# Thirty-two dense tokens in place of sixteen take their U activations from fetched rows, and modulation dots move out of layer 0's V stage

## The chip, the cores and the metric

The kernel runs on one core of one Trainium2 chip. The metric is the device time of one execution in microseconds, as the median of several runs; lower is better. Engines are named as in the profile: PE multiplies matrices (PEld is its weight load), DVE is the vector engine, ACT the scalar engine, POOL is GpSimd, SP (SyncE) issues DMAs.

## The reference, cut to what matters

A trunk of two layers works on 512 tokens of width 1024 in float32. Layer 0 mixes with an mLSTM and a gated convolution, layer 1 with stick-breaking attention; both are conditioned by modulation vectors (`ada_params`, one dot of length 1024 for each of 6144 values a layer). After each mixer comes the channel mixer, which is where nearly all of the time goes:

```python
def peer_ffn(h, w_query, sub_keys1, sub_keys2, expert_u, expert_v):
    # 8 heads, 16 picks each: 128 of 16384 experts a token
    ...
    expert = e1 * PEER_NKEYS + e2
    gate = jax.nn.softmax(top_v.astype(jnp.float32), axis=-1).astype(h.dtype)
    ...
    def block(args):
        xt, et, gt = args
        act = jax.nn.gelu(jnp.einsum("td,thkd->thk", xt, expert_u[et]), approximate=False) * gt
        return jnp.einsum("thk,thkd->td", act, expert_v[et])
```

The expert tables U and V have 16384 rows of 1024 floats, 64 MB each.

## The kernel before

**Two ways to do the channel mixer.** For the 384 "dense" tokens (DENSE_T) the kernel multiplies the whole table: in the U stage 128 tiles of U (each 128 experts, 512 KB) meet the tokens' h, the gelu of all activations is stored to DRAM (gel_dram), and in the V stage 128 tiles of V meet the activations times the gates, most of which are zero. Floats are split into a high and a low part, so each product is three matmuls (high by high, high by low, low by high). For the last 128 tokens, "fetched", the 128 picked rows of U and V are gathered by indirect DMA, one row for each token at a time (128 partitions, one token each), and DVE computes a dot (U) or adds a scaled row (V).

**The dense tokens with fetched U rows.** The last EXTRA = 16 of the dense tokens take no part in the U matmuls: their width is DENSE_U = 368. Their activations come from fetched rows as well, 16 gathers of 128 partitions (8 groups of picks by 16 tokens). SP spreads their picks and shares over the groups (`spread_extra`), ACT copies their h out of PSUM (L1185) and SP copies it to the other groups (`copy_extra`); DVE's dots read it as h_extra, from SBUF (`dot`, L2355), where the fetched tokens' h lies in PSUM (h_rows, shown as gbank). The activations get gelu, share and a transpose (L2413), 8 small DMAs (`gather_extra`) bring them into place, and they then act as the gates of these tokens, for which gel holds ones. In V these tokens are like all other dense ones.

**The U stage by engine.** A tile is 8 steps of three matmuls (L1364 to L1366). ACT rounds the raw tile to w_hi (L840), w_lo is the rest, by POOL (L737) nearly to the end of U, afterwards and in V by DVE (L2315), always two tiles or more ahead. ACT takes the gelu out of PSUM (L1114). Beside the first 26 tiles (U_EARLY) DVE picks the experts (L2249 to L2307). From tile 26 on the gate matrices are made beside the tiles: DVE's one-hots (L2326) and planes (L2331) and ACT's low planes (L1153) of four tokens, PE's gate pairs of two tokens (L1745, at places that `pair_step` writes into the tiles' steps), ACT's copy (L1163) and DVE's sum (L2340) into stage, which goes to g_dram in pieces. PE turns h into rows at tiles 27 and 28 (`turn_extra`, `turn_h` L1718), the latter once ACT has copied h_extra. From ROWS_FROM = 27 on `rows_of(n)` says which dots DVE does in tile n: 23 in 18 tiles, the 28 first for fetched tokens, then the 16 extra ones. POOL issues the fetch three dots ahead and after the split of the tile (`peer`, `u_fetch` L759), in order: a fetch waits until a dot has freed one of four buffers, and the next split waits behind it. So 129 of the 144 dots are done in U.

**The V stage by engine.** A tile is 18 matmuls of 512 columns (L1384). For each, DVE does the split (L2315), the product of gel and gates (L2385, L2386), one fetched row's addition (L2369) and the low part of the product (L2394); ACT rounds (L840, L1177). SP loads the raw tile, and gates and gel in units of four tiles. The 15 dots that are left stand in tiles 2, 8, ..., 86 (`dot_beside`); at Z_AT = 88 the second part of z gets its gelu. In layer 0 twenty dots of layer 1's modulation stand in the same tiles 6i + 2 (`mod_dots`), each with a load of 512 KB by ACT; in layer 1 eight others stand in tiles 98 + 3i. Sixteen more modulation dots stand beside the q and k tiles of layer 1 (`dots_of`, L1888), 3 in two tiles.

SP's queue issues loads in a hand-written order and waits for w_lo's semaphore before each (`load_after`).

Of the kernel before, what the change touches and what calls it, by code (L numbers as in the profile page):

```python
# [263 lines left out]
def build(nc, stream, x_t, c, ada, ada_b, gains, gate_b, conv_w, mnorm, keys, qk_norm, u0, v0, u1, v1, out_t):  # L264
# [275 lines left out]
    def _(sp_):  # L540
# [101 lines left out]
        def gather_extra(layer, q):  # L642

            if q == 0:
                sp_.wait_ge(S("extra_by_dve"), counted(layer)["extra_by_dve"] + GATES_TURNED)
            at = 2 * EXTRA * (q // 2)
            sp_.dma_start(gate_extra[picks_of(q), :], turned_extra[at:at + EXTRA, picks_of(q % 2)]
                          ).then_inc(S("extra_moved"), 16)

        done = RING  # L650
        for layer in range(2):
# [1933 lines left out]
```

## Time and profile before

| what | value |
|---|---|
| median of 3 runs | 2995.73 us (2993.57 to 3000.06) |
| the profiled execution | 2994.8 us, span 2993.1 us |
| granted TensorE clock | 0.999 |
| PE busy | 2955.0 us (99%) |
| DVE busy | 2568.7 us (86%) |
| POOL busy | 1682.4 us (56%) |
| ACT busy | 1534.0 us (51%) |
| DMA | 863.94 MB, mean 289 GB/s |
| U stage of layer 0, of layer 1 | 382 to 950 us, 1894 to 2461 us |
| V stage of layer 0, of layer 1 | 951 to 1474 us, 2461 to 2983 us |

The profile is of one execution, and its times are microseconds from the span's start. A row with "x" gives the count of instructions. "busy" of an engine in a window is the union of its instructions' times; instructions overlap by their pipelines, so means add up to more than the union. The DMA share is the mean over the 16 engines of the time that their packets took, which can pass 1. The chain of work is followed back from the last instruction, at each step to what released it.

### The profile page before, as it was taken

Reading aid. Unit: us, or ns where it says so; the run is one execution under the profiler, and the core shown is the slowest. Engines: PE = TensorE matmul, PEld = TensorE weight load, DVE = VectorE, ACT = ScalarE, POOL = GpSimd, SP = SyncE. Lnnn points to the kernel's source line nnn. Section 1 sums busy time; section 2 is a strip of 40 time slices with the busy share of each in tenths; the row PEclk is TensorE's granted clock in tenths of the full one; section 3 lists DMA queues with packets and bytes.
Section 4 is the critical chain, followed back from the end, with each engine's and each line's share of the span. In section 5 each row is a group of like instructions: output and inputs, shape, how many; then the busy total and the mean of one; then the engine's idle time right before and its main releaser. Section 6 shows DMA issues by size and latency. Waiting matters only on the chain.

```text
span 2993.1 us, 45300 instructions
## 1 busy us (share of the span) xinstructions
PE 2955.0 (99%) x15526; PEld 2623.1 (88%) x15526; DVE 2568.7 (86%) x5068; ACT 1534.0 (51%) x2866; POOL 1682.4 (56%) x1010
## 2 busy tenths in 40 slices
PE   8999999999999999999999999999999999999999
PEld 6788899999999888888788788999999998888887
DVE  7887998898988999898754949998998889888897
ACT  6345345776775333343465743347777763333332
POOL 4334358798776554453255534587887875523222
PEclk9999999999999999999999999999999999999999
DMA  7623246999999999999554512459999999999996
GB/s 285 238 100 109 82 162 222 357 338 385 368 354 389 393 394 393 391 378 389 202 190 134 120 64 85 143 200 333 353 369 373 366 381 387 392 372 370 347 379 258
DMA packets 327201, 863.94 MB, mean 289 GB/s; under 512 B 30480, under 2 KB 151328, under 8 KB 326992
## 3 DMA queue, kind: packets, MB, share of 16 engines
q1 hardware_dynamic: 191936, 438.81, 41.2%
q0 software_dynamic: 78608, 285.58, 25.3%
q10 hardware_dynamic: 56448, 136.86, 12.1%
q8 instruction: 119, 1.95, 0.3%
q14 instruction: 90, 0.74, 0.1%
HBM read 752.69 MB, written 94.90 MB: 283 GB/s over the span
## 4 chain that ended last, share of the span: by engine, by line
PE 65%; DVE 22%; ACT 4%; DMA 4%; POOL 2%; issue 2%; ACTq 0%; DVEq 0%; POOLq 0%; SPq 0%
PE banks L1384 22%; PE gbank L1384 11%; PE banks L1364 5%; PE banks L1365 5%; PE banks L1366 5%; PE banks L1344 3%; PE banks L1346 3%; PE banks L1345 3%; DVE u_rows L2355 2%; DVE hot L2326 2%; DMA raw<-stream_dram 2%; DVE pick L2283 2%; POOL w_lo L737 1%; PE gbank L1745 1%; DVE pick L2278 1%
## 5 line engine op out<-in xcount | busy, mean ns | idle before, releaser
L737 POOL TENSOR_TENSOR w_lo<-raw,w_hi 128x1024 fp32r<-128x1024 f32 x355 | 908.3, 2562 | 480.4 <-ACT w_hi L840 476.8
L840 ACT ACTIVATE w_hi<-raw 128x1024 fp32r<-128x1024 f32 x613 | 646.2, 1054 | 568.2 <-PE banks L1384 285.1
L767 POOL DMA_INDIRECT v_rows<-v_dram,row_of x256 | 391.0, 1527 | 573.8 <-DVE fetched L2369 558.9
L1364 PE MATMUL banks<-h_hi,w_hi 128*128 128x368 f32 x2048 | 674.8, 329 | 0.0
L1365 PE MATMUL banks<-h_lo,w_hi 128*128 128x368 f32 x2048 | 672.9, 329 | 0.0
L1366 PE MATMUL banks<-h_hi,w_lo 128*128 128x368 f32 x2048 | 672.9, 329 | 0.0
L1364 PEld LDWEIGHTS banks<-h_hi,w_hi 128*128 128x128 f32 x2048 | 384.4, 188 | 0.6 <-POOL w_lo L737 0.5
L1365 PEld LDWEIGHTS banks<-h_lo,w_hi 128*128 128x128 f32 x2048 | 384.3, 188 | 0.0
L1366 PEld LDWEIGHTS banks<-h_hi,w_lo 128*128 128x128 f32 x2048 | 384.1, 188 | 0.0
L759 POOL DMA_INDIRECT u_rows<-u_dram,row_of x256 | 258.4, 1009 | 163.8 <-DVE z L2355 127.2
L2369 DVE SCALAR_TENSOR_TENSOR fetched<-v_rows,share,fetched 128x1024 f32<-128x1024 f32 x254 | 326.2, 1284 | 1.5 <-DMA v_rows<-v_dram,row_of 1.0
L2355 DVE CUSTOM_DVE_ANT_0 u_rows<-u_rows,gbank 128x1024 f32<-128x1024 f32 x256 | 307.2, 1213 | 16.4 <-DMA u_rows<-u_dram,row_of 15.4
L1384 PE MATMUL banks<-w_hi,a_lo 128*128 128x512 f32 x1024 | 315.4, 389 | 0.0
L1384 PE MATMUL banks<-w_hi,a_hi 128*128 128x512 f32 x1024 | 315.3, 389 | 0.0
L1384 PE MATMUL banks<-w_lo,a_hi 128*128 128x512 f32 x1024 | 315.2, 389 | 0.0
L2315 DVE TENSOR_TENSOR w_lo<-raw,w_hi 128x1024 fp32r<-128x1024 f32 x258 | 313.9, 1217 | 0.0
L1153 ACT ACTIVATE plane<-hot,gate_lo 128x128 fp32r<-128x128 f32 x768 | 246.3, 392 | 123.6 <-DVE hot L2326 84.3
L1344 PE MATMUL banks<-h_hi,w_hi 128*128 128x512 f32 x672 | 266.9, 397 | 1.0 <-POOL w_lo L737 1.0
L1346 PE MATMUL banks<-h_hi,w_lo 128*128 128x512 f32 x672 | 262.3, 390 | 0.0
L1345 PE MATMUL banks<-h_lo,w_hi 128*128 128x512 f32 x672 | 262.1, 390 | 0.0
L2326 DVE TENSOR_TENSOR hot<-banks,exT 128x1024 fp32r<-128x1024 f32 x192 | 233.9, 1218 | 4.0 <-PE gbank L1745 2.4
L1384 PEld LDWEIGHTS banks<-w_hi,a_lo 128*128 128x128 f32 x1024 | 192.2, 188 | 40.0
(403 smaller groups left out, 5105.2 us busy)
## 6 DMA issues: line engine op xcount, KB each, us to landing
raw<-stream_dram SPq DMA_DIRECT2D x613, 512.0 KB, 7.3
gel_dram<-gel ACTq DMA_DIRECT2D x248, 192.0 KB, 5.3
gin<-gel_dram SPq DMA_DIRECT2D x62, 768.0 KB, 11.6
g_dram<-stage ACTq DMA_DIRECT2D x56, 768.0 KB, 11.2
gates<-g_dram SPq DMA_DIRECT2D x64, 672.0 KB, 7.8
ada_w<-ada_dram ACTq DMA_DIRECT2D x44, 512.0 KB, 7.6
ada_first<-ada_dram SPq DMA_DIRECT2D x8, 1024.0 KB, 17.8
ada_more<-ada_dram ACTq DMA_DIRECT2D x16, 512.0 KB, 4.8
```

What stands on the lines that cost most here:

```text
L737: pool.tensor_tensor(w_lo[:, s, :], raw[:, s, :], w_hi[:, s, :].bitcast(F32), ALU.subtract).then_inc(split_lo, 1)
L767: pool.indirect_dma_start(v_rows[:, j % V_ROWS, :], None, (v0, v1)[layer], bass.IndirectOffsetOnAxis(ap=row_of[:, j:j + 1], axis=0)).then_ ...
L840: act.activation(w_hi[:, s, :], raw[:, s, :], ACT.Copy).then_inc(split_hi, 1)
L1344: pe.matmul(out, wh, hi(k), start=(k == 0), stop=False)
L1345: pe.matmul(out, wh, lo(k), start=False, stop=False)
L1346: mm = pe.matmul(out, wl, hi(k), start=False, stop=(k == DC - 1))
L1364: pe.matmul(out, wh, h_hi[:, k, 0:DENSE_U], start=(k == 0), stop=False)
L1365: pe.matmul(out, wh, h_lo[:, k, 0:DENSE_U], start=False, stop=False)
L1366: mm = pe.matmul(out, wl, h_hi[:, k, 0:DENSE_U], start=False, stop=(k == DC - 1))
L1384: mm = pe.matmul(sums[c][half][:], a, w[:, half * SEQ:(half + 1) * SEQ], start=(v == 0 and a is ah and w is hi), stop=(v == NKEYS - 1 and ...
L2355: dve.tensor_tensor_reduce(row, row, h, 1.0, 0.0, ALU.mult, ALU.add, to).then_inc(S("dotted"), 1)
L2369: add = dve.scalar_tensor_tensor(out=fetched[:], in0=row, scalar=share[:, j:j + 1], in1=fetched[:], op0=ALU.mult, op1=ALU.add)
```

## The change

EXTRA becomes 32, so the U matmuls have 352 columns, there are 4 groups of picks, 32 extra dots, and 160 dots a layer. `rows_of` does five in four tiles (126 in U), and the 34 left stand in V tiles 2, 4, 7, 9, ..., 84 (`dot_tile`). With 32 tokens DVE's transpose in blocks of 32 puts each group's values where they belong, so the 8 gather DMAs, their wait and the zeroed columns go, and EXTRA_HI and EXTRA_LO come 6 and 8 tiles after the last extra dot. Layer 0's V stage keeps 12 modulation dots, in tiles 94 to 121, and 24 stand beside q and k, two in each tile from 2 to 13.

```diff
-EXTRA = 16
+EXTRA = 32
...
-Z_HALF = 96
+Z_HALF = 94
...
-    return range(min(U_SUMS, 23 * (n - ROWS_FROM) // 18), min(U_SUMS, 23 * (n - ROWS_FROM + 1) // 18))
+    return range(min(U_SUMS, 5 * (n - ROWS_FROM) // 4), min(U_SUMS, 5 * (n - ROWS_FROM + 1) // 4))
...
-EXTRA_GEL, EXTRA_TURN, EXTRA_LOAD, EXTRA_HI, EXTRA_LO = (EXTRA_DONE + n for n in (2, 4, 13, 26, 28))
+EXTRA_GEL, EXTRA_TURN, EXTRA_HI, EXTRA_LO = (EXTRA_DONE + n for n in (2, 4, 6, 8))
...
-V_DOT_EVERY = 6
+
+
+def dot_tile(i):
+
+    return 2 + 5 * i // 2
 
 
 def dot_beside(v):
 
-    i, r = divmod(v - 2, V_DOT_EVERY)
-    return U_DOTS + i if r == 0 and 0 <= i < PICKS - U_DOTS else None
+    beside = [U_DOTS + i for i in range(PICKS - U_DOTS) if dot_tile(i) == v]
+    return beside[0] if beside else None
...
-    return range(3 * (m - 2) // 2, 3 * (m - 1) // 2) if 2 <= m < 13 else range(0)
+    return range(2 * m - 4, 2 * m - 2) if 2 <= m < 14 else range(0)
...
-OUT_DOTS, V_DOTS, QKV_DOTS, LATE_DOTS = 4, 20, 16, DC
+OUT_DOTS, V_DOTS, QKV_DOTS, LATE_DOTS = 4, 12, 24, DC
...
-    at = ([6 * i + 2 for i in range(V_DOTS)], [98 + 3 * i for i in range(LATE_DOTS)])[layer]
+    at = ([94 + 5 * i // 2 for i in range(V_DOTS)], [98 + 3 * i for i in range(LATE_DOTS)])[layer]
...
-            for q in range(GROUPS_OF_PICKS):
-                gather_extra(layer, q)
-                load_after(done_to + q)
...
                 if n == EXTRA_HI:
-                    act.wait_ge(S("extra_moved"), past["extra_moved"] + EXTRA_OUT)
-                    act.activation(gate_extra_hi[:], gate_extra, ACT.Copy).then_inc(S("extra_by_act"), 1)
+                    act.wait_ge(S("extra_by_dve"), past["extra_by_dve"] + GATES_TURNED)
+                    act.activation(gate_extra_hi[:], gate_extra[:], ACT.Copy).then_inc(S("extra_by_act"), 1)
...
-                    link(dve.tensor_tensor(z_extra[:, 0:EXTRA], z_extra[:, 0:EXTRA], share_extra[:], ALU.mult))
-                    dve.transpose(turned_extra[:], z_extra[:]).then_inc(S("extra_by_dve"), 1)
+                    link(dve.tensor_tensor(z_extra[:], z_extra[:], share_extra[:], ALU.mult))
+                    dve.transpose(gate_extra[:], z_extra[:]).then_inc(S("extra_by_dve"), 1)
```

## Rows read from the trace of the kernel before

**Rows 1.** The page, the chain that ended last: share of the span by engine

```profile
PE 65%; DVE 22%; ACT 4%; DMA 4%; POOL 2%; issue 2%; ACTq 0%; DVEq 0%; POOLq 0%; SPq 0%
```

**Rows 2.** Windows, L1364 alone, the last L1384: us, PE busy, PEld, clock, DMA, GB/s

```profile
394.00:474.00 80.00, 52.57 (x161) 30.01 (x160) 1.00 0.53 180
...
725.00:747.00 22.00, 12.12 (x37) 6.76 (x36) 1.00 1.02 398
767.00:857.00 90.00, 53.01 (x162) 30.25 (x161) 1.00 0.98 365
...
1043.20:1288.00 244.80, 244.80 (x1082) 202.78 (x1081) 1.00 1.03 391
```

**Rows 3.** Matmuls of L1364 and L1384 by line (ns min/median/max), L1745 in the chain

```profile
L1364 PE MATMUL banks<-h_hi,w_hi x2048: 325/329/441, 382.3 to 2459.6; 128*128 128x368 f32 x187
...
L1384 PE MATMUL banks<-w_hi,a_hi x1024: 388/389/398, 952.1 to 2982.2; 128*128 128x512 f32 x171
...
749.93 0.24 PE gbank L1745 x2
```

**Rows 4.** The chain in order of time, and PE's timeline at 497.57 (layer 0)

```profile
496.50 1.02 ACT h_extra L1185
...
497.57 0.33 PE L1718 MATMUL gbank<-ident_r,h_hi 128*128 128x128 f32 x1 [0.43 <-ACT h_extra L1185]
...
730.43 13.21 DMA u_rows<-u_dram,row_of
```

**Rows 5.** POOL's timeline among the extra dots: start, us, instruction, idle before

```profile
604.68 1.76 POOL L759 DMA_INDIRECT u_rows<-u_dram,row_extra  x1 [0.16 <-issue]
...
609.04 1.76 POOL L759 DMA_INDIRECT u_rows<-u_dram,row_extra  x1 [0.16 <-issue]
...
628.65 1.76 POOL L759 DMA_INDIRECT u_rows<-u_dram,row_extra  x1 [0.16 <-issue]
630.71 0.94 POOL L759 DMA_INDIRECT u_rows<-u_dram,row_extra  x1 [0.30 <-issue]
...
634.25 1.76 POOL L759 DMA_INDIRECT u_rows<-u_dram,row_extra  x1 [0.16 <-issue]
```

**Rows 6.** DVE's dots by line L2355, ns min/median/max

```profile
L2355 DVE CUSTOM_DVE_ANT_0 u_rows<-u_rows,gbank x256: 1203/1212/1225, 499.7 to 2811.8; 128x1024 f32<-128x1024 f32 x128
...
L2355 DVE CUSTOM_DVE_ANT_0 u_rows<-u_rows,h_extra x32: 1214/1522/2106, 600.0 to 2167.1; 128x1024 f32<-128x1024 f32 x32
```

**Rows 7.** Windows counting L737, then L1364; PE's wait in 640:672; POOL's timeline

```profile
0.00:592.40 592.40, 277.73 (x104) 1.00 0.54 193
...
0.00:599.05 599.05, 131.76 (x400) 75.06 (x400) 1.00 0.55 194
...
PEld banks L1364 <- POOL w_lo L737: 0.2, 1, 0.2
...
596.73 0.94 POOL L759 DMA_INDIRECT u_rows<-u_dram,row_extra  x1 [3.28 <-DVE z L2355]
```

**Rows 8.** Windows: us, busy of PE, PEld, DVE, ACT, POOL, clock, DMA share, GB/s

```profile
1060.00:1300.00 240.00, 240.00 (x1061) 198.80 (x1060) 221.18 (x336) 88.96 (x118) 120.46 (x67) 1.00 1.03 390
2560.00:2800.00 240.00, 240.00 (x1061) 198.73 (x1060) 213.47 (x319) 87.86 (x119) 82.80 (x68) 1.00 1.00 373
```

**Rows 9.** Waits in V: 1060:1300, 2560:2800, 955:1000 (total, times, longest); GB/s in 40 slices

```profile
ACT w_hi L840 <- DMA raw<-stream_dram: 72.8, 30, 5.9
...
ACT w_hi L840 <- DMA raw<-stream_dram: 23.7, 8, 4.4
...
PEld gbank L1384 <- DVE w_lo L2315: 1.9, 2, 1.2
...
GB/s 401 407 372 406 385 393 411 371 407 400 377 409 373 404 409 371 404 390 390 409 371 408 405 374 408 375 403 406 372 404 393 387 386 376 399 326 374 408 355 397
```

**Rows 10.** DVE's timeline beside the k tiles

```profile
1576.61 1.27 DVE L2469 TENSOR_TENSOR qsq_lo<-qsq,qsq_hi 128x512 fp32r<-128x512 f32 x1 [1.54 <-ACT qf L1281]
...
1587.11 3.43 DVE L1888 CUSTOM_DVE_ANT_0 ada_mid<-ada_mid,cvec 128x1024 f32<-128x1024 f32 x1
```

More of the change, by code:

```diff
@@ L107 @@
 EXTRA_COPIED = 16 * (GROUPS_OF_PICKS - 1)
-EXTRA_OUT = EXTRA_COPIED + 16 * GROUPS_OF_PICKS
 H_ROWS_COPIED, GELU_TAKEN, GATES_ROUNDED = 1, 2, 3
@@ L111 @@
 assert quad_step(EXTRA_QUAD - 2) > DC * EXTRA_LO
-V_DOT_EVERY = 6
+def dot_tile(i):
+    return 2 + 5 * i // 2
 def dot_beside(v):
-    i, r = divmod(v - 2, V_DOT_EVERY)
-    return U_DOTS + i if r == 0 and 0 <= i < PICKS - U_DOTS else None
-Z_AT = V_DOT_EVERY * (PICKS - U_DOTS - 1) + 4
+    beside = [U_DOTS + i for i in range(PICKS - U_DOTS) if dot_tile(i) == v]
+    return beside[0] if beside else None
+Z_AT = dot_tile(PICKS - U_DOTS - 1) + 2
 assert Z_AT < Z_HALF
@@ L167 @@
           "exT": 5, "hot": QUADS, "one": QUADS, "one_lo": QUADS, "gate_lo": 1, "g_mm": PAIRS_OF_TOKENS, "g_hi": PAIRS_OF_TOKENS, "g_out": PAIRS_OF_TOKENS, "stored0": 16 * PIECES * ((STORED + 1) // 2), "stored1": 16 * PIECES * (STORED // 2), "picked": 3,
-          "h_rows": 2, "u_row": 16 * U_SUMS // U_ROWS, "extra_in": EXTRA_IN, "extra_moved": EXTRA_OUT, "extra_by_act": 3, "extra_by_dve": 2, "v_row": 16 * PICKS // V_ROWS, "dotted": U_SUMS, "z_gel": 2,
+          "h_rows": 2, "u_row": 16 * U_SUMS // U_ROWS, "extra_in": EXTRA_IN, "extra_moved": EXTRA_COPIED, "extra_by_act": 3, "extra_by_dve": 2, "v_row": 16 * PICKS // V_ROWS, "dotted": U_SUMS, "z_gel": 2,
           "added": PICKS, "acc": DENSE_C - 1, "y_rows": 2 * DENSE_C, "turned": DC,
@@ L291, in build @@
     rowsel = sb("rowsel", [LOW_ROW + HEADS, HEADS, P], F32R)
+    iota_at = place[0]
     iota = sb("iota", [P, P])
@@ L443, in build @@
     share_extra = sb("share_extra", [P, EXTRA])
-    z_extra = sb("z_extra", [P, 2 * EXTRA])
-    gate_extra = z_extra[:, 0:EXTRA]
-    turned_extra = sb("turned_extra", [P, 2 * EXTRA])
     u_end = place[0]
+    place[0] = rowsel_at + DENSE_T * 4
+    z_extra = sb("z_extra", [P, EXTRA])
+    gate_extra = sb("gate_extra", [P, EXTRA])
+    assert place[0] <= iota_at
     place[0] = share_at
@@ L640, in copy_extra @@
             sp_.dma_start(h_extra[picks_of(q), :], h_extra[0:EXTRA, :]).then_inc(S("extra_moved"), 16)
[L642 to L648, printed above, removed]
         done = RING
@@ L670, in _ @@
                 load_after(done_to + q - 1)
-            loads(done_to + GROUPS_OF_PICKS - 1, DENSE[layer] + EXTRA_LOAD)
-            done_to = DENSE[layer] + EXTRA_LOAD
-            for q in range(GROUPS_OF_PICKS):
-                gather_extra(layer, q)
-                load_after(done_to + q)
-            loads(done_to + GROUPS_OF_PICKS, DENSE[layer] + FIRST_UNIT_AT + UNIT_LEAD)
+            loads(done_to + GROUPS_OF_PICKS - 1, DENSE[layer] + FIRST_UNIT_AT + UNIT_LEAD)
             for s in range(2):
@@ L1188, in peer @@
                     act.wait_ge(S("dotted"), past["dotted"] + EXTRA_FROM + EXTRA)
-                    act.activation(z_extra[:, 0:EXTRA], z_extra[:, 0:EXTRA], ACT.Gelu).then_inc(S("extra_by_act"), 1)
+                    act.activation(z_extra[:], z_extra[:], ACT.Gelu).then_inc(S("extra_by_act"), 1)
                 if n == EXTRA_HI:
-                    act.wait_ge(S("extra_moved"), past["extra_moved"] + EXTRA_OUT)
-                    act.activation(gate_extra_hi[:], gate_extra, ACT.Copy).then_inc(S("extra_by_act"), 1)
+                    act.wait_ge(S("extra_by_dve"), past["extra_by_dve"] + GATES_TURNED)
+                    act.activation(gate_extra_hi[:], gate_extra[:], ACT.Copy).then_inc(S("extra_by_act"), 1)
                 for i in range(PIECES):
@@ L2416, in peer @@
                     dve.tensor_copy(high_part[:, DENSE_U:], gate_extra_hi[:].bitcast(F32))
-                    dve.tensor_tensor(gate_lo[:, DENSE_U:], gate_extra, gate_extra_hi[:].bitcast(F32), ALU.subtract
+                    dve.tensor_tensor(gate_lo[:, DENSE_U:], gate_extra[:], gate_extra_hi[:].bitcast(F32), ALU.subtract
                                       ).then_inc(S("extra_by_dve"), 1)
```

1 line of the change is left out of this document (removed).

## The prediction

> **What bounds the kernel now.** I read the chain of work that ended last first: 65% of it is PE, 22% DVE [rows 1]. Then windows of the U stage by its matmul line, which give the pace of a tile (a U tile is 8 groups of three matmuls, and L1364 is one of the three). Until tile 26 of a layer 160 matmuls of L1364 begin in 80 us, so a tile takes 4.00 us; later, beside the gate pairs, 161 or 162 in 90 us, so 4.48 us [rows 2]. PE is busy without a break there. In the V stage 18 matmuls of 512 columns make a tile; 1082 of them touch a window of 244.8 us in which PE is busy throughout, 60 tiles of 4.08 us [rows 2]. So wherever PE sets the pace, the width of its operand is the price. What the reader is to look for next is where something else sets it: the first tiles of U, the stretch of the fetched dense tokens, and the transfers of V.
>
> **Narrower U matmuls.** A matmul of 368 columns takes 329 ns and one of 512 takes 389 ns [rows 3]: 60 ns for 144 columns, 0.417 ns a column. Sixteen columns fewer are 6.7 ns, 24 matmuls a tile 0.16 us, 256 tiles 41.0 us. The weight load cannot hold this back: gate matmuls of 256 columns, each with its own weights, follow one another at 0.12 us [rows 3], and the new spacing of a U matmul is 0.160 us.
>
> Not all of it arrives. **First 27 tiles of each layer:** beside them DVE picks the experts, and this chain is on the path to the end: the picks, one-hots, planes, then ACT's copy of h_extra from 496.50, for which PE waits 0.43 us before it turns h [rows 4]. A PE that comes 27 x 0.16 = 4.3 us earlier waits 4.3 us longer. Saved there: 0. **Last three tiles:** no gate pairs, DVE has splits, dots and the first V products to do, and PE waits for it at V's first tile already; I count 0. Left are 98 tiles a layer: 2 x 98 x 0.16 = **31.4 us gained**.
>
> **Tiles that wait for ACT's planes.** The planes of a quad follow the gelu of a tile, so their time counts from the tile's end. In two short stretches of each layer (tiles 28 to 32 and 78 to 82) they are late: 37 L1364 matmuls in 22 us, 4.76 us a tile [rows 2]. There only the steps behind the wait shrink, about half the tile: 20 tiles x 0.08 = **1.6 us lost** (0 to 4, if the next phase of the pattern joins).
>
> **The fetched dense tokens (32 for 16).** A dot against h_extra reads two SBUF operands: median 1522 ns, up to 2106, against 1212 for a dot with PSUM's rows [rows 6]. It hits POOL too, which issues the fetches and splits the U tiles beside it. In the stretch of these dots POOL's fetch takes 1.76 us where it takes 0.94 otherwise, and from 604.68 to 609.04 a tile with one fetch costs POOL 4.36 us; a tile with two costs the 2.06 from 628.65 and the 3.54 from 630.71, 5.60 [rows 5]. The Trainium skill (SBUF — State Buffer, section SBUF: two separate sides) says the same of the mechanism: DVE with two SBUF inputs and GpSimd take an exclusive lock, and the loser waits for the whole instruction. The trace agrees in kind (0.94 to 1.76), and it is the rule that speaks against this change, which doubles such dots.
>
> Before, 13 tiles of one fetch and 5 of two give (13 x 4.36 + 5 x 5.60)/18 = 4.70 us a tile against PE's 4.48, for 12.5 tiles. POOL had a lead: its 104th split, that of U tile 50 (53 tiles come before U), is done by 592.4, and PE has begun 50 U tiles (400 matmuls) by 599.05, so 6.65 us; it is used up to a wait of 0.2 us around 652 [rows 7]. That is more than the 12.5 x 0.22 = 2.8 us, because the first tile of two fetches also waits 3.3 us for DVE's dot; behind that wait the lead is some 3.5 us. After, three tiles of one fetch and one of two give (3 x 4.36 + 5.60)/4 = 4.67 against PE's 4.32, for 32/1.25 = 25.6 tiles: 9.0 us, less a lead of about 3.1 after the same wait, is 5.9 us a layer, **11.8 us lost** on both. Bounds: 3 a layer, if a slower PE spreads dots and fetches so that they meet less often; 10 a layer, if the loss goes on as fast as between 599 and 652 (6.5 us in 12 tiles at 4.48, so 0.54 + 0.16 for 25.6 tiles, 17.9 less the wider lead of 6.65, rounded down).
>
> Three dots fewer in U (126 for 129), eight small gather transfers less, the wider transposes and ACT's copy of 32 rows for 16 (the free size is the same): 0. The removed gathers stood in SyncE's queue with a wait, but between loads that have slack; two fewer pairs of spreads likewise. A row of u that arrived late is on the chain to the end once in the gated stretch of layer 0 (13.2 us from issue to use, at 730.43 [rows 4]); a tile moved 365 x 4.48 = 1.635 MB [rows 2] and will move 0.028 rows of 0.524 MB less in 4.32 us, 375 GB/s, so such rows come no sooner: **1 us lost** (0 to 4).
>
> **V: 34 dots for 15, in every 2.5th tile for every 6th.** DVE has room: in 240 us (59 tiles) with a third of a dot and modulation dot a tile it is busy 221 [rows 8]; 0.4 a tile adds 0.07 x 1.3 = 0.1 us to 3.75, below 4.08. The transfers have none. In layer 0, V moves 390 GB/s at a DMA share of 1.03 [rows 8], and ACT waits for raw tiles 30 times, 72.8 us, against 8 times, 23.7, in layer 1 at 373 [rows 9]: 390 is nearly all that this mix gets through. One tile moves 390 x 4.08 = 1.59 MB, a third of it of a row (0.524 MB) for dots. After, 0.4 of a row: 1.59 + 0.067 x 0.524 = 1.626 MB, 399 GB/s, in both layers until tile 86. If 392 to 394 is the limit, a tile takes 4.14 us: 0.06 x 72 tiles = 4.3 us in each layer once the start is over; the start itself (in layer 0 PE's weight loads wait 1.9 us for DVE's splits [rows 9]; layer 1 has no such row) repeats in layer 0 and costs layer 1 some 1.9. Sum: **10.5 us lost**. Bounds: 4, if the mix reaches 396; 15, if 390. Layer 0's twelve modulation dots from tile 94 on ask the same 399 for 28 tiles, but eight tiles without any come ahead, which win back more than they take: 0. Between the ends of this term I stay near the middle, as layer 0's own row is the nearest.
>
> **Eight more dots beside q and k.** DVE idles 1.54 us ahead of a q/k step and has dots of up to 3.43 us against POOL's splits [rows 10]; two dots in each of twelve steps fit but for the last ones: **0.5 us lost** (0 to 2). The last dot that ACT's first gelu of z needs is now that of U's last tile; ACT waits at that point for a product that DVE makes behind it anyway: 0.
>
> **Sum**, against the profiled execution's 2994.8 us (span 2993.1): -31.4 + 1.6 + 11.8 + 1.0 + 10.5 + 0.5 = -6.0, so 2988.8; the median of the runs is 2995.7, 0.9 above the profiled time, and I say 2988.5, 0.24% below the median. A difference of 0.2% (6 us) is about what a measurement of this kernel can tell from none.
>
> **The rivals.** (1) Transfers and POOL absorb more: V has slices of 407 and 411 GB/s [rows 9], above the 399 needed. If these can be held, V loses 1 to 4, and with 3 a layer on POOL the time is 2994.8 - 31.4 + 1.6 + 6 + 3 = 2974. The mean over 240 us beside a waiting ACT speaks against it. The Trainium skill (DMA: Bandwidth & Descriptors, Specifications) gives 435 GB/s for the fabric, which would make V free, and 358 for the HBM share of a core, which the 390 measured here already exceed. (2) The lock decides: POOL falls behind by 0.7 us a tile for the 25.6 tiles, 17.9 us less a lead of 6 to 8, so 10 a layer, DVE's late dots hold its fetches, and V is at its upper bound: 2994.8 - 31.4 + 1.6 + 20 + 15 + 2 = 3002, slower than before. It decides as soon as POOL's tile in that stretch costs more than 5.0 us. For it speaks the fast loss of the lead before; against it that most fetches there met a dot already (4.36 is the price with the collision in every tile). (3) PE gains nothing in the gated stretch because ACT's planes become the pace everywhere: 98 tiles x 0.08 lost a layer, 2994.8 - 15.7 + 12 + 10.5 + 1.5 = 3003. The planes have margin in all but two stretches (4.48 exactly), so this is unlikely.
>
> **Chances.** The sum as forecast (2981 to 2996) 0.55; rival 1 0.25; rival 2 0.13; rival 3 0.04; anything else 0.03. The range that holds 8 in 10 goes from 2974 to 3000. Faster by over 0.2% (below 2989.7): all of rival 1 and a little over half of the forecast's own range, 0.54; within 0.2%: 0.33, the rest of the forecast's range and the near edge of rivals 2 and 3; slower: 0.13.
>
> **What would show it.** Ungated U tiles at 3.84 us and gated ones at 4.32; PE's wait ahead of L1718 grown from 0.4 to some 4.7 us; in the tiles 55 to 75 of U a tile of 4.6 to 4.7 us, with PE waiting for POOL's w_lo in both layers; V tiles before 86 at 4.10 to 4.16 at 390 to 396 GB/s, with ACT waiting for raw in both layers, and 4.08 behind. Wrong would be a U matmul spacing other than 0.160 us, V tiles at exactly 4.08 (rival 1), or U tiles of 5 us beside h_extra (rival 2).

## The result and the profile after

The changed kernel takes 3004.16 us (median; 2998.61 to 3010.59), beside 2995.11 for the kernel before in the same job: a ratio of 1.0029, with an interval of 1.0020 to 1.0038. It is slower, by 9 us. The forecast was 2988.5 us, and the range ended at 3000. The same kernel in another job (p4 below) came out at 1.0010 [1.0001, 1.0019], so its cost lies between 0.1 and 0.3%. Stretches of about 100 us differ by 2 to 3 us from one execution of the same kernel to the next, so what is read from one profile below is held against the second one, p4, and against the other kernels that have the same tiles.

The profiled execution took 3007.84 us, its span 3006.1. From the page of the profile after: busy time, the chain that ended last by engine, and two of the costliest groups (busy us, mean ns | idle us just before, releaser).

```profile
PE 2934.4 (98%) x15526; PEld 2592.3 (86%) x15526; DVE 2621.5 (87%) x5130; ACT 1532.2 (51%) x2866; POOL 1739.4 (58%) x1042
...
PE 40%; DVE 26%; DMA 19%; POOL 8%; issue 4%; ACT 2%; SPq 0%; ACTq 0%; DVEq 0%; POOLq 0%
...
L832 ACT ACTIVATE w_hi<-raw 128x1024 fp32r<-128x1024 f32 x613 | 645.5, 1053 | 449.3 <-DMA raw<-stream_dram 344.0
...
L1356 PE MATMUL banks<-h_hi,w_hi 128*128 128x352 f32 x2048 | 666.3, 325 | 12.9 <-POOL w_lo L729 8.6
```

Against [rows 1] PE falls from 65% of the chain to 40%, DMA rises from 4 to 19, POOL from 2 to 8: the matmuls did get shorter, and the chain went to what stands beside them. Where PE sets the pace it keeps the predicted one. The windows of the ungated and of the gated U tiles, the first U matmul line alone (L1356 now; us, PE busy and count, PEld, clock, DMA, GB/s), hold 168 groups in 80 and in 90 us where [rows 2] has 161 and 162:

```profile
394.00:474.00 80.00, 53.71 (x168) 31.40 (x167) 1.00 0.56 190
...
767.00:857.00 90.00, 54.01 (x168) 31.56 (x167) 1.00 0.98 369
```

I then cut both spans at the same milestones of PE (the starts of the weight loads of certain U and V tiles). "mid" runs from V tile 127 of layer 0 to the first U tile of layer 1, with q and k in it. The forecast's column is what its own terms say for that stretch.

```
us                 layer 0: before  after  diff | layer 1: before  after  diff | forecast, both | p4's diff, layer 0, 1
to first U tile             382.3   382.6   0.4 |                              |   0            |  -0.3
U tiles 0-27                117.3   118.3   1.0 |          117.3   117.2  -0.1 |   0            |  -1.9  -1.5
U tiles 28-48                95.0    91.9  -3.1 |           95.0    92.0  -3.1 |  -5.9          |  -3.1  -2.0
U tiles 49-76               125.7   129.4   3.7 |          125.2   130.6   5.4 |   3.8          |   1.7   2.3
U tiles 77-84                37.7    38.3   0.6 |           37.6    38.3   0.6 |  -1.8          |   2.1   0.6
U tiles 85-124              178.9   172.6  -6.4 |          178.9   172.6  -6.4 | -12.8          |  -5.1  -5.6
U tile 125 to V              13.6    17.0   3.3 |           13.1    17.7   4.7 |   0            |   2.4   4.5
V tiles 0-11                 50.6    50.5  -0.1 |           48.9    50.5   1.6 |   1.9          |  -0.2   1.5
V tiles 12-85               301.9   304.1   2.2 |          301.9   305.0   3.1 |   8.6          |   2.0   5.3
V tiles 86-126              167.3   167.3   0.0 |          167.3   167.3   0.0 |   0            |   0.6   0.0
mid / tail                  423.4   428.2   4.8 |           14.0    14.9   0.9 |   0.5          |   4.6   0.9
```

The sum is +13.0 where the forecast says about -6 (the medians differ by 9). Four rows make nearly all of that gap: the last tiles of U (8.0), the tiles of the fetched dense tokens (5.2), "mid" (4.3) and tiles 77 to 84 (2.9). V comes out 3.7 cheaper than forecast. In p4 the sum is +8.9, and three of the four come again (7.0, 4.1 and 4.5), but the fetched dense tokens cost 4.0 us there, where 3.8 was forecast: that row's excess is mostly scatter between executions.

**The clock.** The trace of before has the granted clock at 0.5 (1.2 GHz of 2.4) for 3.41 us from 31.0 and at the very end. The trace of after has these two and seven more between: from 486.0 (6.83 us long), 704.5, 950.2, 1492.9, 1591.9, 2004.9 and 2469.2. PE's timeline around the second one:

```profile
484.17 0.66 PE L1723 MATMUL gbank<-ident,ex 128*128 128x128 f32 x4 [0.97 <-DVE ex L2276]
486.92 1.12 PE L1723 MATMUL gbank<-ident,ex 128*128 128x128 f32 x4 [2.10 <-DVE ex L2282]
...
488.72 0.49 PE L1356 MATMUL banks<-h_hi,w_hi 128*128 128x352 f32 x1
489.01 0.49 PE L1357 MATMUL banks<-h_lo,w_hi 128*128 128x352 f32 x1
489.30 0.49 PE L1358 MATMUL banks<-h_hi,w_lo 128*128 128x352 f32 x1
...
493.16 0.33 PE L1357 MATMUL banks<-h_lo,w_hi 128*128 128x352 f32 x1
493.32 0.32 PE L1358 MATMUL banks<-h_hi,w_lo 128*128 128x352 f32 x1
```

PE has waited 0.97 and 2.10 us for DVE's picks, and then its matmuls start 0.29 us apart instead of 0.16. From 486.92 to 493.00 PE does four turns and 18 matmuls, which take 3.37 us at full clock in p4 (from 484.50): 2.7 us lost, and some 1.6 for a stretch of 3.41. All seven would be some 12 us, if PE set the pace in each. The Trainium skill (TensorE: Matmul & The Clock Gate, HAM oscillation — how this bites in real kernels) prices throttled time at half of itself, by which I estimate 3.4 us for the 6.83 here; the trace has 2.7, as PE stood idle for the first 0.9 us of them.

### The profile page after: what moved, and what is told of

It is laid out like the page before. It is cut to its first block, busy times and chain, and to the rows that moved or that the text cites. A ratio compares the mean times of both kernels' runs of the same rounds, so it can differ in the third digit from the quotient of the medians.

```text
span 3006.1 us, 45456 instructions
## 1 busy us (share of the span) xinstructions
PE 2934.4 (98%) x15526; PEld 2592.3 (86%) x15526; DVE 2621.5 (87%) x5130; ACT 1532.2 (51%) x2866; POOL 1739.4 (58%) x1042
## 3 DMA queue, kind: packets, MB, share of 16 engines
q8 instruction: 119, 1.95, 0.3%
## 4 chain that ended last, share of the span: by engine, by line
PE 40%; DVE 26%; DMA 19%; POOL 8%; issue 4%; ACT 2%; SPq 0%; ACTq 0%; DVEq 0%; POOLq 0%
DMA raw<-stream_dram 16%; PE banks L1376 7%; POOL w_lo L729 4%; PE banks L1356 4%; PE banks L1357 4%; PE banks L1358 4%; DVE w_lo L2306 4%; PE gbank L1376 3%; POOL u_rows L751 3%; PE banks L1336 3%; PE banks L1338 3%; PE banks L1337 3%; DVE fetched L2360 2%; DVE u_rows L2346 2%; DMA u_rows<-u_dram,row_of 2%
## 5 line engine op out<-in xcount | busy, mean ns | idle before, releaser
L759 POOL DMA_INDIRECT v_rows<-v_dram,row_of x256 | 384.7, 1503 | 548.5 <-DVE fetched L2360 540.1
L1356 PE MATMUL banks<-h_hi,w_hi 128*128 128x352 f32 x2048 | 666.3, 325 | 12.9 <-POOL w_lo L729 8.6
L1357 PE MATMUL banks<-h_lo,w_hi 128*128 128x352 f32 x2048 | 662.9, 324 | 0.0
L1358 PE MATMUL banks<-h_hi,w_lo 128*128 128x352 f32 x2048 | 662.7, 324 | 0.0
L1356 PEld LDWEIGHTS banks<-h_hi,w_hi 128*128 128x128 f32 x2048 | 388.3, 190 | 17.1 <-POOL w_lo L729 10.9
L751 POOL DMA_INDIRECT u_rows<-u_dram,row_of x256 | 268.0, 1047 | 148.0 <-DVE z L2346 102.6
L1169 ACT ACTIVATE a_hi<-gin 128x384 fp32r<-128x384 f32 x248 | 129.5, 522 | 303.5 <-DVE gin L2377 302.4
```

What stands on the lines that cost most here:

```text
L751: pool.indirect_dma_start(u_rows[:, j % U_ROWS, :], None, (u0, u1)[layer], bass.IndirectOffsetOnAxis(ap=own, axis=0)).then_inc(S(f"u_row{j ...
L759: pool.indirect_dma_start(v_rows[:, j % V_ROWS, :], None, (v0, v1)[layer], bass.IndirectOffsetOnAxis(ap=row_of[:, j:j + 1], axis=0)).then_ ...
L1356: pe.matmul(out, wh, h_hi[:, k, 0:DENSE_U], start=(k == 0), stop=False)
L1357: pe.matmul(out, wh, h_lo[:, k, 0:DENSE_U], start=False, stop=False)
L1358: mm = pe.matmul(out, wl, h_hi[:, k, 0:DENSE_U], start=False, stop=(k == DC - 1))
```

## The experiments

Twelve runs, in three jobs: m1 to m4, n1 to n4, p1 to p4. Theory A, the forecast's own, mended in size: the lock between DVE's dots of two SBUF operands and POOL costs more than forecast, and the rest is transfers. Theory B: short waits of PE, which the narrower matmuls lengthen, make the clock fall. Theory C: the modulation dots that were moved are what costs.

**m1, the kernel before with only the modulation dots moved.**

```diff
-OUT_DOTS, V_DOTS, QKV_DOTS, LATE_DOTS = 4, 20, 16, DC
+OUT_DOTS, V_DOTS, QKV_DOTS, LATE_DOTS = 4, 12, 24, DC
-    at = ([6 * i + 2 for i in range(V_DOTS)], ...
+    at = ([94 + 5 * i // 2 for i in range(V_DOTS)], ...
```

> The kernel before with the modulation dots alone moved: 12 from tile 94 of layer 0's V on, 24 beside q and k. In the changed kernel this section (from the last V matmuls of layer 0 to layer 1's U) took 4.8 us longer: PE waited 2.1 us for a square-sum operand of DVE at 1591, and the granted clock was 0.5 for the 3.4 us after it. If the section's loss comes from the move, this kernel shows that wait and that stretch and is 3 to 5 us slower than the kernel before, less up to 2 us for layer 0's V stage, where the modulation loads no longer meet the start (PE stood 1.9 us there). Rival: the section's loss belongs to the later arrival of the V stage's end; then this kernel is within 1 us of before.

Measured: 2996.68 us, ratio 1.0005 [0.9996, 1.0014]. No difference by itself, but two opposite ones inside: "mid" is 427.3 for 423.4, and the first V tiles of layer 0 are 48.9 for 50.6. PE's timeline of m1 beside the last k tile:

```profile
1584.01 0.39 PE L1346 MATMUL banks<-h_hi,w_lo 128*128 128x512 f32 x1
1586.50 0.77 PE L1780 MATMUL gbank<-qsq_hi,half_r 128*128 128x512 f32 x1 [2.10 <-issue]
1587.07 0.63 PE L1781 MATMUL gbank<-qsq_lo,half_r 128*128 128x512 f32 x1
1587.49 0.63 PE L1344 MATMUL banks<-h_hi,w_hi 128*128 128x512 f32 x1
```

A wait of 2.10 us, and behind it matmuls of 0.63 us for 0.39: half clock. The same in after, where DVE's and POOL's timelines say whom PE waits for:

```profile
1586.30 2.30 DVE L1880 CUSTOM_DVE_ANT_0 ada_mid<-ada_mid,cvec 128x1024 f32<-128x1024 f32 x1
1588.53 0.08 DVE L1880 DVE_READ_ACCUMULATOR2_ANT mod<- 128x1 f32 x1
1588.53 2.83 DVE L2460 TENSOR_TENSOR qsq_lo<-qsq,qsq_hi 128x512 fp32r<-128x512 f32 x1
```

```profile
1587.48 6.12 POOL L729 TENSOR_TENSOR w_lo<-raw,w_hi 128x1024 fp32r<-128x1024 f32 x2
```

```profile
1591.46 0.47 PE L1772 MATMUL gbank<-qsq_hi,half_r 128*128 128x512 f32 x1 [2.08 <-issue]
...
1592.06 0.63 PE L1336 MATMUL banks<-h_hi,w_hi 128*128 128x512 f32 x1
```

The kernel before has two dots ahead of this qsq_lo as well (2.30 and 1.62 us), but one in the step before it, and DVE idles 1.54 us there [rows 10]; with two dots in every step it has not idled since 1563. So DVE comes later to qsq_lo, which then takes 2.83 us beside POOL's two splits. In before, the same step:

```profile
1582.61 1.77 DVE L2469 TENSOR_TENSOR qsq_lo<-qsq,qsq_hi 128x512 fp32r<-128x512 f32 x1
```

PE starts 0.1 us after qsq_lo's end at 1591.36. The move of the dots costs 3.9 us in "mid" and gives 1.7 back at V's start.

**m2, the changed kernel with the modulation dots left where they were** (m1's diff the other way round).

> The changed kernel with the modulation dots where they were (20 in V, 16 beside q and k), so the 32 dense tokens and the new order of dots alone. If the parts add up, it is the changed kernel less 3 to 5 us for q and k, plus what 20 modulation dots cost in layer 0's V, which then asks 0.4 + 0.17 rows a tile, 421 GB/s at 4.08 us. If the transfers of that mix have their limit near 400 GB/s, V of layer 0 takes 4.3 us a tile up to tile 86, 15 to 20 us more; if the limit is above 420, it stays at 4.08 and the kernel comes to 2999 to 3001. The second outcome would say that my limit of 392 to 394 was no limit at all.

Measured: 3015.11 us, 1.0069 [1.0052, 1.0086], 11 us above the changed kernel (15 above p4). V tiles 12 to 85 of layer 0 take 320.7 us for 304.1. Window, and waits, of that stretch in m2:

```profile
1000.00:1290.00 290.00, 278.45 (x1200) 224.55 (x1199) 265.27 (x407) 100.43 (x133) 127.26 (x93) 0.99 1.04 394
...
PEld gbank L1376 <- DVE w_lo L2306: 19.6, 20, 3.3
```

and in after (both layers, then the waits in 1000:1300):

```profile
1000.00:1290.00 290.00, 288.37 (x1272) 238.15 (x1271) 265.14 (x405) 105.94 (x139) 125.41 (x97) 1.00 1.03 392
2520.00:2820.00 300.00, 298.73 (x1311) 245.34 (x1310) 273.58 (x419) 109.41 (x143) 130.30 (x99) 1.00 1.03 390
...
ACT w_hi L832 <- DMA raw<-stream_dram: 103.5, 46, 8.1
...
PEld gbank L1376 <- DVE w_lo L2306: 2.5, 2, 1.9
```

With a sixth of a modulation row more in each tile the stream does not go beyond 394 GB/s, and PE pays: this is the limit the forecast read out of [rows 8, 9]. DVE is as busy in after (265.14 us of the 290) without holding PE up, so it is not DVE's load. So theory C falls as the main cause. Alone, the move costs nothing, and together with the new dots it saves 11 to 15 us; the two parts need each other.

**m3, the extra dots against PSUM's rows.** The extra tokens are dotted with the rows of h that the other dots use, in PSUM, in place of h_extra in SBUF; their activations are then those of other tokens. Counts, order, fetches and waits stay.

```diff
-                h, to = (h_extra[:], z_extra[:, e:e + 1]) if is_extra(j) else (h_rows, z[:, m:m + 1])
+                h, to = (h_rows, z_extra[:, e:e + 1]) if is_extra(j) else (h_rows, z[:, m:m + 1])
```

> The changed kernel, but the 32 extra dots of a layer read the fetched tokens' h in PSUM instead of the extra tokens' h in SBUF: the same number of dots and fetches, and only the operand's place differs (the extra tokens' activations are then those of other tokens). If the port that DVE and POOL share makes the stalls of U's tiles 60 to 76, POOL's fetches take 0.95 us everywhere, no PE wait for POOL's w_lo is left there, the halved clock at 704 is gone, and the kernel is 14 to 20 us faster than the changed one (8.7 us a layer from those tiles, some more from tiles 78 to 84). Rival: the number of dots and fetches is what DVE and POOL cannot carry at 4.32 us a tile; then most of the stalls stay and the gain is under 5 us.

Measured: 2986.72 us, 0.9967 [0.9955, 0.9979], 17 us below the changed kernel (14 below p4). U tiles 49 to 76 take 120.8 and 121.3 us for 129.4 and 130.6. POOL's timeline in that stretch, first after, then m3:

```profile
663.95 1.76 POOL L751 DMA_INDIRECT u_rows<-u_dram,row_extra  x1 [0.16 <-issue]
665.72 2.44 POOL L729 TENSOR_TENSOR w_lo<-raw,w_hi 128x1024 fp32r<-128x1024 f32 x1
668.32 1.76 POOL L751 DMA_INDIRECT u_rows<-u_dram,row_extra  x1 [0.16 <-issue]
```

```profile
659.50 0.95 POOL L751 DMA_INDIRECT u_rows<-u_dram,row_extra  x1 [0.16 <-issue]
660.47 2.41 POOL L729 TENSOR_TENSOR w_lo<-raw,w_hi 128x1024 fp32r<-128x1024 f32 x1
663.04 0.95 POOL L751 DMA_INDIRECT u_rows<-u_dram,row_extra  x1 [0.16 <-issue]
```

A tile costs POOL 4.37 us (663.95 to 668.32) in the one and 3.54 (659.50 to 663.04) in the other. And PE, windows 640 to 700, first after, then m3:

```profile
640.00:700.00 60.00, 57.05 (x360) 55.04 (x359) 57.37 (x81) 39.13 (x100) 53.04 (x29) 1.00 0.95 355
```

```profile
640.00:700.00 60.00, 60.00 (x391) 60.00 (x390) 55.15 (x89) 43.64 (x112) 50.71 (x32) 1.00 0.98 374
```

With the second SBUF operand gone PE does not stop at all in these 60 us, and the transfers go faster too. So this one operand costs 14 to 17 us, more than the whole loss: theory A holds for this stretch, and the number of dots and fetches, its rival, costs nothing there (120.8 and 121.3 us for 28 tiles of 4.32). Nor is it the clock: m3's trace has five falls between start and end too, 23.9 us of half clock where after has 27.3. It is also what the Trainium skill says (SBUF — State Buffer, SBUF: two separate sides): two SBUF inputs of a DVE instruction are one of the cases in which it and a GpSimd instruction that reads SBUF exclude each other. The trace agrees with 0.95 against 1.76 us.

**m4, the changed kernel with matmuls that fill PE's waits** (fillers): 5 and 9 behind tile 25 while DVE picks, 6 before V's first tile. They write to banks that are not in use then.

```diff
+                for _ in range((0, 5, 9)[n]):
+                    pe.matmul((None, misc[1], misc[3])[n][:], ident_r[:], h_hi[:, 0, :], start=True, stop=True)
...
+            for _ in range(6):
+                pe.matmul(bank[2][:], ident[:], xT[:, 0, :], start=True, stop=True)
```

> The changed kernel with matmuls that nobody reads put into PE's two long waits: 14 of 512 columns while it waits for the picks at U tile 25, and 6 in float32 before V's first tile. If the granted clock falls because PE stands idle there, the stretches of clock 0.5 at 486, 950, 2005 and 2469 are gone; they cost 3.4 + 3 x 1.7 = 8.5 us of PE time, of which I expect 4 to 7 back (the first tiles then wait for the copy of h_extra instead). Rival: the clock falls whatever PE does; then the kernel is 0 to 3 us slower than the changed one, by the matmuls added.

Measured: 3001.32 us, 1.0016 [1.0006, 1.0027]. The stretches of half clock at 486, 950, 2005 and 2469, the four behind filled waits, are all gone; those of "mid" remain, and the one at 704.5 is replaced by two, at 736.8 and 2252.4, behind waits of 2.07 and 2.06 us. Window 486 to 492.8 of after and of m4:

```profile
486.00:492.80 6.80, 5.88 (x21) 5.88 (x22) 4.74 (x10) 2.79 (x9) 3.29 (x4) 0.50 0.49 168
```

```profile
486.00:492.80 6.80, 6.80 (x55) 6.71 (x54) 4.99 (x10) 3.67 (x11) 2.98 (x3) 1.00 0.63 216
```

So PE's waits make the clock fall here, and all fourteen profiles bear it out. Behind the last turn of the picks PE waits 2.10 us in after, n1 and n3, and the clock falls in all six cases; where that wait is 0.7 or 0.8 us (p4, m2, m3, p1) it falls in none of eight. At V's first tile it waits 2.8 to 3.7 us with the narrow matmuls, and the clock falls in 11 of 14 cases; with the old width (before, m1, p2, n2) it waits 0.8 to 1.9 us, and it falls in none of eight. With these waits filled (m4, n4, p3) it falls in none of twelve. This is theory B's mechanism.

What it costs m4 does not measure. The profiled span is 7.7 us shorter, near the 7.5 of the four stretches, but only 2.5 us of that lie where they were: 1.7 up to U tile 27 and 2.6 in V tiles 0 to 11, less 1.9 from tile 125 to V. The medians differ by 3 us, their intervals overlap, and against p4 (3000.33) nothing is left. For the fillers outlast the waits:

```profile
944.70 5.31 PE L1760 MATMUL banks<-xT,ident 128*128 128x512 f32 x12
949.45 1.02 PE L1376 MATMUL gbank<-w_hi,a_hi 128*128 128x512 f32 x2
```

```profile
946.98 0.45 ACT L1106 ACTIVATE gel<-banks 128x352 f32<-128x352 f32 x1
```

V's first tile waits for ACT's last gelu. In after it starts 0.2 us behind it, in m4 2.0 us behind it in both layers, and the last turn of the picks in layer 0 starts 2.4 us after DVE has made them. Theory B is right as a mechanism; its cost is at most some 12 us and stays open. In the eight runs of the changed kernel the mean granted clock does not order the times: 0.993 goes with 3002.5 and 3004.2 us, 0.996 with 3010.4.

**n1, the extra dots at every second place** (from 28 on), so that each has a PSUM dot between.

```diff
-    return EXTRA_FROM <= s < EXTRA_FROM + EXTRA
+    return EXTRA_FROM <= s < EXTRA_END and (s - EXTRA_FROM) % EXTRA_STEP == 0
```

> The changed kernel with the 32 extra dots at every second place from dot 28 on, not in one row: the same dots and fetches a tile, and all of them right. If POOL's slowed fetches cost time only because 26 tiles of them come in one run, a mean tile costs POOL about half-way between 4.67 and 3.8 us, 4.2, under PE's 4.32, its lead holds, and U's tiles 49 to 76 take 121 to 123 us in place of 129.4 and 130.6, so the kernel gains 12 to 17 us on the changed one (3004), as the kernel with the operand in PSUM did (2986.7). Rival: DVE and POOL lose the same sum of time in another place, as each such dot still meets a fetch; then the stalls are spread over tiles 49 to 100 and the gain is under 5 us.

Measured: 3004.61 us, 1.0025 [1.0015, 1.0035], the same as the changed kernel. Its profiled execution (3018.87 us) lies 14 us above the median, so I take n3 and n4, which have the same dots, with it: in the three profiles tiles 49 to 76 take 125.2 us in the mean (128.7 in the six profiles with the dots in one row: after, p4, m2, m4, p1, p3), and tiles 85 to 124 take 178.8 (172.6 in after, up to 177.9 in p1). The cost moved with the dots, and a lead of POOL does not carry it.

**n2, the changed kernel with U matmuls of 368 columns again** (the 16 more are not read).

```diff
-            out = bank[t % 2][:, 0:DENSE_U]
+            wide = DENSE_T - 16
+            out = bank[t % 2][:, 0:wide]
```

> The changed kernel with U matmuls of 368 columns as before: 16 columns are computed that nobody reads, and all else is the change. It separates what the narrower matmuls give from what the dots, fetches and moved modulation take. By the terms of the sum 98 tiles a layer are 0.16 us longer, 31.4 us; where POOL sets the pace (tiles 52 to 76) a slower PE costs nothing, 20 tiles a layer at most, and the start of V has its transfers in time again, 3 to 4 us a layer. So 3004 + 31 - 6 to 10 (POOL) - 4 to 8 (start of V) - 2 to 4 (halved clock) = 3013 to 3023. Against the kernel before (2996) this would be the price of the dots and their order, 17 to 27 us. Rival: the narrower matmul gives back less than 10 us because the gated stretch is not PE's; then the kernel is within 3 us of the changed one.

Measured: 3016.19 us, 1.0069 [1.0050, 1.0087]. So everything that the change adds costs 19 to 21 us at the old width, less than the 23.8 that the forecast took off for it, and the narrow matmuls give back 12 (16 against p4) of the 31.4 that they are shorter: it is the gain that is missing. This kernel also shows what happens at U's end. Windows from 900 us to the first V tiles, before, after (to 953) and n2:

```profile
900.00:965.00 65.00, 63.66 (x369) 60.92 (x368) 51.21 (x88) 37.01 (x79) 43.70 (x32) 1.00 1.01 389
```

```profile
900.00:953.00 53.00, 48.38 (x296) 47.02 (x296) 41.62 (x72) 31.03 (x71) 37.73 (x28) 0.97 1.02 393
```

```profile
900.00:965.00 65.00, 63.62 (x374) 61.37 (x373) 53.28 (x91) 39.21 (x84) 44.79 (x32) 1.00 1.02 395
```

The stream is at or near m2's 394 in all three, before V begins. PE needs 13.7 us from tile 125 to V in n2 and 13.6 in before, 17.0 in after: what 40 tiles had gained (6.4) is half handed back, because a faster PE does not make the transfers faster. The chain of after names them (start, us):

```profile
925.55 16.02 DMA raw<-stream_dram
...
949.03 7.74 DMA v_rows<-v_dram,row_of
```

and PE's wait there, in 945 to 1000:

```profile
PE gbank L1376 <- ACT gel L1106: 2.9, 1, 2.9
```

A load of raw takes 16.02 us from issue to landing, where their median is 8.0. ACT's gelu stands behind the rounding that waits for it, and PE behind the gelu; in before the same wait is 1.3 us.

**n3, n1 with four more modulation dots in V and four fewer beside q and k; n4, n1 with m4's fillers.**

```diff
-OUT_DOTS, V_DOTS, QKV_DOTS, LATE_DOTS = 4, 12, 24, DC
+OUT_DOTS, V_DOTS, QKV_DOTS, LATE_DOTS = 4, 16, 20, DC
-    at = ([94 + 5 * i // 2 for i in range(V_DOTS)], ...
+    at = ([90 + 2 * i for i in range(V_DOTS)], ...
```

> The kernel with the spread extra dots and the modulation dots laid out anew: 16 of them in V tiles 90 to 120, every second, and 20 beside q and k, five in three steps, for 12 and 24. If DVE's lag behind q and k (PE waited 2.1 us at 1591 and then had 3.4 us of half clock) comes from two dots in each of twelve steps, this wait is gone and the section from V to U takes 424 to 425 us for 428, 3 to 4 us less than the kernel it is made from. V's tiles 86 to 127 ask 412 GB/s for 31 tiles, over the 394 that the transfers reach, but raw tiles have a lead of some 8 us by then: 0 to 2 us. Rival: the section's loss comes from the norm at its head, not from the dots; then 428 stays.

> The same as the kernel before it in this list with the matmuls of m4_warm in PE's waits for the picks and before V. Filling the waits took away the clock's fall at both places in m4_warm and gave 2.9 us; if that adds up, this kernel is 1 to 4 us faster than without them, 2982 to 2988. Rival: without the stalls of U the clock falls less often and the fillers cost their own time; then it is equal or slower.

Measured: n3 3008.42 us, 1.0038 [1.0024, 1.0051]; n4 3013.65 us, 1.0058 [1.0044, 1.0073]. Neither helps. In n3 "mid" is 428.2 all the same, and V tiles 86 to 126 of layer 0 take 171.9 us for 167.3; that the closer dots there do it is not shown, as n1 and n4, whose dots stand there as in after, have 170.7 and 172.4. n4 is 9 us above n1, although n1's falls at 486, 2008 and 2472 are gone. Its fillers outlast the waits for the picks in both layers, by 2.4 and 2.5 us, and those at V's starts by 1.8 and 1.7; the rest of the 9 us stays open.

**p1, p2, p3, the loads for V's first units two tiles later and with two loads of raw between them**, in the changed kernel (p1), the kernel before (p2) and m4 (p3); **p4, the changed kernel again.**

```diff
-UNIT_LEAD = 6
+UNIT_LEAD = 4
-            load_after(units_from)
+            for t in range(units_from, units_from + 2):
+                load_after(t)
```

> The changed kernel with the three unit loads ahead of V (2 x 672 KB of gates, 768 KB of gel) issued from two tiles earlier on and with two raw tiles between them, not one. In the changed kernel the last three U tiles and the way into V took 17.0 and 17.7 us for 13.6 and 13.1, ACT waited 10.3 us for raw tiles there, and one raw load took 16.0 us. If transfers crowded together at that place take back what narrower matmuls saved, this kernel needs 13.5 to 15.5 us there and is 3 to 6 us faster than the changed one. Rival: V's start is bound by DVE's late dots and the gelu behind them; then 17 to 18 us stay.

> The same move of the unit loads in the kernel before, whose way into V took 13.6 and 13.1 us with one wait of 13.6 us for a raw tile on the chain. If the crowding matters only at the faster pace of U, it is within 0.1% of the kernel before; if there too, it is 1 to 3 us faster.

> The changed kernel with both the earlier unit loads and the matmuls in PE's waits (m4_warm). If the two add up: 3001.3 less 3 to 6, so 2995 to 2998, level with the kernel before (2997). If the fillers only helped because V started late, nothing is added to the first kernel of this list.

> The changed kernel itself once more, for a second profile and more times beside the others of this list: 3002 to 3006. It tells which of its stretches of halved clock come again (486, 704, 950, 1493, 1592, 2005 and 2469 before) and which are of one execution. If a long wait of PE decides, those after the waits for the picks, for V's start and for q and k's square sums come again, as their waits do.

Measured: p1 3006.88 us, 1.0035 [1.0022, 1.0047]; p2 2998.75 us, 1.0011 [1.0002, 1.0020]; p3 3009.13 us, 1.0035 [1.0021, 1.0048]; p4 3000.33 us, 1.0010 [1.0001, 1.0019]. In p1 the way from tile 125 to V shrinks as meant, to 15.5 and 15.4 us, and tiles 85 to 124 grow from 172.6 to 176.9 and 177.9, as PE now stalls in tiles 122 and 123. The sum of the two is 192 to 193 us, as in before, and 190 in after. So this other order of the loads brings nothing. Its stream is not full in 900:953, though:

```profile
900.00:953.00 53.00, 46.93 (x264) 44.90 (x263) 38.00 (x66) 26.53 (x59) 32.87 (x24) 0.90 0.99 366
```

It carries 366 GB/s for 393 in after, so that no order of these loads could do better is not shown. p3 does not add p1 and m4 up; it is not faster than either. p4 has the clock falls of "mid" and of both V starts, two others at 734.9 and 2011.5, and none at 486, where its picks were ready earlier: PE waits 0.8 us for them, and 1.3 for ACT's copy of h_extra. Such chances differ between executions, and with them a few us.

None of the versions that compute the whole result was faster than the kernel before.

## Why the prediction was wrong

**Narrower U matmuls: size and place right, the arrival not.** The spacing is 0.160 us, tiles 28 to 48 gain 3.1 us a layer and tiles 85 to 124 gain 6.4, as worked out (2.0 and 5.1 in the least of p4's). But n2 shows that of 31.4 us only 12 to 16 reach the end.

**"Last three tiles: I count 0" is the step that failed most.** It took PE's wait there for one on DVE and looked no further; the wait at V's first tile is for ACT's gelu behind a late load of raw, 1.3 us before and 2.9 after, and the stream on the way there carries 389 GB/s in before already. I had used that limit for V and not for the end of U. It cost 3.3 and 4.7 us (2.4 and 4.5 in p4), and n2 (13.7 and 14.2 us at the old width) shows that it is the narrow matmuls' own gain.

**The fetched dense tokens: mechanism right, and the size nearly.** POOL's tile of one fetch is 4.37 us as forecast from [rows 5] (4.36). Against PE's own pace the stretch costs 3.7 + 4.5 = 8.2 us in layer 0 and 9.9 in layer 1, where 5.9 was said and 10 was the bound. But p4 has 6.2 and 6.8, and the six profiles with these tiles have 127.0 to 132.1 us, 128.7 in the mean, which is 7.7. The waits in layer 0 of after (tiles 49 to 76, 592.8 to 722.2: total, times, longest) show of what:

```profile
PEld banks L1356 <- POOL w_lo L729: 5.7, 4, 2.1
PE banks L1356 <- POOL w_lo L729: 4.5, 4, 1.8
```

POOL takes 4.5 to 5.7 of the 8.2, and the half clock at 704.5, behind such a wait, some 1.6.

**Tiles 77 to 84: the turn that was priced at 0.** They take 38.3 us for 37.7, where 0.9 fewer was said. It is not ACT's planes: these tiles take the 4.7 us that the forecast asks for, but tile 80 takes 6.6. PE waits 2.03 to 2.05 us there for DVE's stage (at 740.3 and 2257.8 in after, 734.7 in p4). The change brings the product of z_extra and its shares and the transpose behind it from DVE's tile 65 to its tile 78, into the stretch whose planes are late, and ahead of the one-hots in DVE's queue. The product is 128x32 and has two SBUF operands, so it stands behind POOL's split. DVE, then POOL, of m3:

```profile
720.91 2.57 DVE L2403 TENSOR_TENSOR z_extra<-z_extra,share_extra 128x32 f32<-128x32 f32 x1
```

```profile
721.02 2.41 POOL L729 TENSOR_TENSOR w_lo<-raw,w_hi 128x1024 fp32r<-128x1024 f32 x1
```

It ends 0.05 us after the split, and so it does in after and p4, where it is 0.63 and 1.95 us long, behind waits of DVE for a late row of u (3.34 and 1.96 us). That is why m3, which frees only the dots, keeps this wait (38.0 and 38.3 us), and why n1, whose turn comes in tile 103, has none in tile 80 (4.7 us). m1's 38.3 and 38.4 us come from another tile, 82 (5.8 us), and why is open. "The wider transposes: 0" had the work right and its place wrong.

**V: sign right, 6.8 us for 10.5, above the lower bound of 4.** 304.1 and 305.0 us for 74 tiles are 4.11 and 4.12 us, at 392 and 390 GB/s; 4.14 at 392 to 394 was said, and m2 puts the limit at 394. They are not tiles of an even 4.14 but of 4.08 with a few that stall. In layer 0 the whole loss is one stall, at tile 70 (5.99 us, and 4.48 for the next), behind a load of raw that takes twice the median:

```profile
1224.16 15.79 DMA raw<-stream_dram
```

So the mix nearly fits: in m4 the same tiles lose 0.4 and 0.3 us at 393 and 391 GB/s, in p4 2.0 and 5.3. Tiles 86 to 126 are unchanged, as said.

**Beside q and k: 4.8 us for 0.5, beyond the bound of 2.** The step "two dots in each of twelve steps fit but for the last ones" is true for time and not for order: the dots stand ahead of qsq_lo in DVE's queue, they use up the idle time of the steps before, and both meet POOL's splits. m1 shows 3.9 us, of which 2.1 is the wait and 1.6 the half clock behind it.

**The clock was in no term.** Two of the four rows that failed contain such a stretch (704.5 in tiles 49 to 76, 1492.9 and 1591.9 in "mid"), and so do U tiles 0 to 27 and V tiles 0 to 11. By the trace it is up to 12 us; m4's median gives back 3 or none of the 7.5 that were taken away, net of what the fillers cost.

**The first 27 tiles.** Saved 0 was said; layer 0 lost 1.0 and layer 1 gained 0.1. The wait grew at the picks (0.97 and 2.10 us), not ahead of the turn of h. Without the fall of the clock, as in p4 (115.4 and 115.8 us), some 2 of the 4.3 us a layer do arrive.

**The rivals.** Rival 2 gave 3002 us, nearest to the measured time, but that is luck, not its mechanism: the tiles of that stretch take 4.62 and 4.66 us in the mean, not the 5.0 that it asked for, V cost half of what it priced, and U's end and q and k, which it had at 0 and 2, made up the sum. A chance of 0.13 for slower was too low, as four costs of one sign stood against one gain and each had been placed near the middle of its own bounds.

**Slips in the sum, none of which decides.** 6.0 off the median of 2995.7 is 2989.7, not 2988.5. The bound of 10 a layer for the dense tokens is 17.9 less 6.65, so 11.3. The lower bound of 4 for V leaves out the 1.9 of its start; at 396 GB/s its own terms give 5.6.

## What to carry over

Shortening the busiest engine's work gives only what the next limit leaves: read the transfer rate in every stretch that is to get faster, not only in the one that gets more bytes, as a stretch at 389 of 394 GB/s gave nothing back here. When DVE work is added, ask which of its operands lie in SBUF while GpSimd works, and what stands behind it in DVE's own queue, even for 32 columns; one PSUM operand was worth 14 to 17 us here, more than the whole change. Before a row of one profile is explained, see whether a second one has it. And look at what PE does behind a new wait of two microseconds, since it may run at half clock for longer than it has waited.

## What the hardware showed that I had not expected

The granted clock fell to 0.5 for 3.41 or 6.83 us inside stages in which PE is busy for 98% of the time, behind waits of 1.8 us (703.5), 2.1 (486.9, 1591.5) and 2.9 (950). The length of the wait alone does not settle it. The wait of 2.05 us for DVE's stage in tile 80 had no fall behind it in after and one in p4 (734.9); 2.84 us at 2448.2 in m3 had none, and 1.35 us at 2010.0 in p4 had one. A wait of 3.06 us at the start of layer 1 (1492.0 in after), the same in all fourteen profiles, has a fall behind it in thirteen, and none in before. With PE kept busy at the picks and at V's starts no fall followed, but I can't tell from these runs which waits make it fall.

The collision of DVE and POOL goes both ways: the fetch grows from 0.95 to 1.76 us, qsq_lo from 0.68 (1576.27) to 2.83, a modulation dot from 1.21 to 3.42 us beside POOL's splits, and a product of 32 columns takes as long as the rest of the split (2.57 us).

At the end of the kernel, behind the last V tile, every version with the change in the tokens takes 14.8 to 15.2 us for 14.0, also at the old matmul width (n2); no run here shows why.
